# Delta rule in a hybrid streaming encoder: the triangular inverse built by whole-array products on the transposed matrix

## What is computed

```python
G = jnp.cumsum(gc, axis=-1)
decay_in = jnp.exp(jnp.where(causal, G[..., :, None] - G[..., None, :], -jnp.inf))
kk = jnp.einsum('nbhid,nbhjd->nbhij', kc, kc)
M = jnp.where(strict, bc[..., :, None] * kk * decay_in, 0.0)
rhs = jnp.concatenate([bc[..., None] * vc, (bc * jnp.exp(G))[..., None] * kc], axis=-1)
sol = lax.linalg.triangular_solve(M + eye, rhs, left_side=True, lower=True)
...
def step(S, xs):
    u = u_v_n - jnp.einsum('bhld,bhdv->bhlv', w_k_n, S)
    o = jnp.einsum('bhld,bhdv->bhlv', q_dec_n, S) + jnp.einsum('bhij,bhjv->bhiv', qk_n, u)
    S = S * g_last_n[..., None, None] + jnp.einsum('bhld,bhlv->bhdv', k_dec_n, u)
```

## Time and profile before

| | |
|---|---|
| three runs | 1804.99, 1807.17, 1808.63 us (median 1807.17) |
| profiled execution | 1809.03 us, of which span 1807.1 us |
| mean granted TensorE clock | 0.97 |
| PE, PEld busy | 93%, 80% of the span |
| DVE, ACT, POOL busy | 59%, 42%, 9% |
| the delta-rule phase | from about 75 us to about 750 us |

### The profile page before, as it was taken

How to read it: one execution, slowest core, us unless ns; L and a number is a source line. 1 busy time by engine, 2 the same in 40 slices (tenths; PEclk the granted TensorE clock), 3 DMA queues, 4 the chain that set the end, 5 groups by cost and what they waited for, 6 DMA issues and landing times. The chain is left out here.

```text
span 1807.1 us, 31679 instructions
## 1 busy us (share of the span) xinstructions
PE 1674.6 (93%) x12005; PEld 1439.7 (80%) x12006; DVE 1066.0 (59%) x2254; ACT 757.6 (42%) x1472; POOL 157.8 (9%) x141
## 2 busy tenths in 40 slices
PE   4799999999999999999998999998999988999990
PEld 2598999999999999887884699998996855666650
DVE  7557857668685875455445311115339976776766
ACT  2555565555556554354444322222113114444434
POOL 0110000000000000100000000000000003444440
PEclk8799999999999999999999999999999989999995
DMA  9521021120202111302116422114123357988866
GB/s 338 184 63 52 25 78 40 52 69 23 79 25 79 39 54 40 117 25 87 61 73 225 169 78 84 46 36 130 48 105 124 143 218 289 322 278 287 246 183 214
DMA packets 69063, 218.09 MB, mean 121 GB/s; under 512 B 9412, under 2 KB 15324, under 8 KB 64324
## 3 DMA queue, kind: packets, MB, share of 16 engines
q1 hardware_dynamic: 61444, 189.02, 29.7%
q0 software_dynamic: 7488, 27.27, 6.3%
HBM read 176.40 MB, written 42.48 MB: 121 GB/s over the span
## 5 line engine op out<-in xcount | busy, mean ns | idle before, releaser
L142 PE MATMUL bk<-hT_high,w_high 128*128 128x352 f32 x840 | 294.9, 351 | 1.1 <-DVE ssq L1303 1.1
L144 PE MATMUL bk<-hT_high,w_low 128*128 128x352 f32 x840 | 272.1, 324 | 0.0
L143 PE MATMUL bk<-hT_low,w_high 128*128 128x352 f32 x840 | 271.8, 324 | 0.0
L142 PEld LDWEIGHTS bk<-hT_high,w_high 128*128 128x128 f32 x840 | 159.7, 190 | 5.3 <-DVE ssq L1303 1.2
L143 PEld LDWEIGHTS bk<-hT_low,w_high 128*128 128x128 f32 x840 | 160.1, 191 | 0.0
L144 PEld LDWEIGHTS bk<-hT_high,w_low 128*128 128x128 f32 x840 | 159.1, 189 | 0.0
L142 PE MATMUL pg<-hT_high,w_high 128*128 128x352 f32 x360 | 116.3, 323 | 0.8 <-PEq L1412 0.8
L143 PE MATMUL pg<-hT_low,w_high 128*128 128x352 f32 x360 | 115.5, 321 | 0.0
L144 PE MATMUL pg<-hT_high,w_low 128*128 128x352 f32 x360 | 115.4, 321 | 0.0
L1084 DVE SCALAR_TENSOR_TENSOR f<-raw,cw,f 128x1059 f32<-128x1059 f32 x72 | 97.1, 1349 | 9.8 <-ACT f L712 8.8
L2730 PE MATMUL psD<-wdn,aTx 128*128 x192 | 86.9, 596 | 2.3 <-DVE ob L2862 1.6
(11 more groups left out here) (489 smaller groups left out, 4149.0 us busy)
## 6 DMA issues: line engine op xcount, KB each, us to landing
wgu<-in_w_gu SPq DMA_DIRECT2D x16, 2048.0 KB, 8.4
wraw<-in_w_gdn SPq DMA_DIRECT2D x32, 512.0 KB, 3.7
wdn<-in_w_dn SPq DMA_DIRECT2D x16, 1024.0 KB, 13.2
wm<-in_w_mod SPq DMA_DIRECT2D x8, 1024.0 KB, 13.3
tmp_x<-x SPq DMA_DIRECT2D x16, 512.0 KB, 3.0
spare<-in_w_mod SPq DMA_DIRECT2D x15, 512.0 KB, 7.9
Dm<-tmp_g_rows SPq DMA_DIRECT2D x8, 576.0 KB, 4.9
EG<-tmp_g_rows SPq DMA_DIRECT2D x8, 576.0 KB, 6.0
```

Source lines behind the costliest of these rows:

```text
L142: pe.matmul(out, lh, rh, start=start, stop=False)
L143: pe.matmul(out, lh, rl, start=False, stop=False)
L144: return pe.matmul(out, ll, rh, start=False, stop=stop)
```

## The change

The inverse is built in another way. C starts as `ET` masked to what lies above the 16x16 diagonal blocks inside each 64x64 quarter (one DVE operation from SBUF, `C_MOFF` changed, no transposes). With the transposed block inverses, the inverse of a quarter is a series in C: Z1 and Z2 each multiply by C and add `RT`, and ZI does the last term for both the inverse (`TT`) and its transpose (`IV`). X and TX make the off-diagonal quarter. All these matmuls have the full 128 rows and 128 columns of weights and 64 moving columns, one per tile, in ZI two. T_ET, BT, B, B2, W, TT and Q are gone; C, Z1, Z2, ZI and X are new, and TX is rewritten. C is the first stage after the slots and waits for `R`. DVE now reads C, Z1, Z2, ZI and X, ACT reads TX, WK and UV. POOL clears two buffers per head. The steps of `fill` are shared out by weights (`SHARE`), 42 in a steady iteration as before. The diff, cut to its core:

```diff
-    A2 = ("QK", "BT", "B", "B2", "W", "TT", "T_O", "Q", "T_V", "TX", "WK", "UV")
+    A2 = ("C", "Z1", "Z2", "ZI", "QK", "T_O", "X", "T_V", "TX", "WK", "UV")
+    SHARE = {"C": 5, "Z1": 5, "Z2": 5, "ZI": 4, "QK": 3, "T_O": 3, "X": 4, "T_V": 3, "TX": 4, "WK": 3, "UV": 4}
...
-    after_stage = {"QK": 2, "W": 3}
+    after_stage = {"C": 2, "QK": 3}
...
+                def zeros(a):
+                    if a > 0:
+                        pool.wait_ge(s["o"], NCHUNK * a)
+                    pool.memset(XL[:, :], 0.0)
+                    pool.memset(IV[:, :], 0.0).then_inc(s["zero"], 1)
...
+                def series(lhsT, rhs):
+                    return lambda t, out: pe.matmul(out, tl(lhsT, t), rhs(t), start=True, stop=True)
                 def inverses(t, out):
-                    mul2(R, A1T)(t, out)
-                    return corner(hl(A1T, 0, t), hl(R, 0, t), out[:, HB2:P], 0)
+                    pe.matmul(out[:, 0:HB2], tl(C, t), ptl(Z2, t), start=True, stop=True)
+                    return pe.matmul(out[:, HB2:P], ptl(Z2, t, P), tl(C, t)[:, 0:HB2], start=True, stop=True)
                 def upper(t, out):
-                    return corner(tl(TT, t)[HALVES[0], HALVES[1]], hl(Q, 0, t), out, 0)
+                    return pe.matmul(out, ptl(XL, t, P), tl(TT, t)[:, HALVES[1]], start=True, stop=True)
...
-                    evacuated(pe, a, "KK")
-                    stage(a, "T_ET", turn(ET))
...
+                    if name == "C":
+                        pe.wait_ge(s["nt"], a + 1)
+                        pe.wait_ge(s["r"], a + 1)
+                        stage(a, "C", series(C, lambda t: htl(R, t)), HB2)
+                    if name == "Z1":
                         pe.wait_ge(s["rt"], a + 1)
+                        stage(a, "Z1", series(C, lambda t: htl(RT, t)), HB2)
+                    if name == "Z2":
+                        stage(a, "Z2", series(C, lambda t: htl(Z1, t)), HB2)
+                    if name == "ZI":
+                        pe.wait_ge(s["zero"], a + 1)
+                        stage(a, "ZI", inverses)
+                    if name == "X":
+                        stage(a, "X", series(ET, lambda t: htl(IV, t)), HB2)
...
-                    for g in range(NGRP):
-                        off_diagonal(a, g)
+                    evacuated(dve, a, "KK")
+                    dve.tensor_tensor(by_tile(C), by_tile(ET), c.consts[:, C_MOFF, :].unsqueeze(1).to_broadcast([P, TILES, P]),
+                                      ALU.mult).then_inc(s["nt"], 1)
...
+                        if name == "C":
+                            for g in range(NGRP):
+                                src = halves(take_from(dve, a, "C", g)[:, 0:G3 * HB2])
+                                dve.tensor_tensor(grp3(C, g)[up, :, up], src[up, :, :], rows_scaled(a, g)[up, :, :], ALU.mult)
+                                dve.tensor_tensor(grp3(C, g)[low_, :, low_], src[low_, :, :], rows_scaled(a, g)[low_, :, :],
+                                                  ALU.mult).then_inc(free[g], 1)
+                        if name == "ZI":
+                            dve.wait_ge(s["r"], a + 1)
+                            for g in range(NGRP):
+                                src = take_from(dve, a, "ZI", g)[:, 0:W3].rearrange("p (t n) -> p t n", n=P)
+                                rt, r = halves(hgrp(RT, g)), halves(hgrp(R, g))
+                                dve.tensor_tensor(halves(hgrp(IV, g))[up, :, :], src[up, :, HB2:P], r[up, :, :], ALU.add)
+                                dve.tensor_tensor(grp3(TT, g)[up, :, up], src[up, :, 0:HB2], rt[up, :, :], ALU.add)
+                                dve.tensor_tensor(grp3(TT, g)[low_, :, low_], src[low_, :, 0:HB2], rt[low_, :, :],
                                                   ALU.add).then_inc(free[g], 1)
```

More of the change, by code:

```diff
@@ L507, in stage_steps @@
         left = start(h + 1) - start(h) - after_slots(h)
-        return left * (i + 1) // len(A2) - left * i // len(A2)
+        upto = [sum(SHARE[name] for name in A2[:n]) for n in (i, i + 1, len(A2))]
+        return left * upto[1] // upto[2] - left * upto[0] // upto[2]
     def subs_done(h, done):
@@ L516, in phase_deltanet @@
         a = h + 1
-        order = ([] if a == HA else ["KK", "T_ET", "SQ", "T_K"]) + \
+        order = ([] if a == HA else ["KK", "SQ", "T_K"]) + \
                 [s for s in A2 if (a < HA or s == "T_O") and (h >= 0 or s != "T_O")]
@@ L585, in hgrp, with htl, pgrp, ptl @@
             return m[:, g * G3 * HB2:(g + 1) * G3 * HB2]
-        def hl(m, b, t):
-            return m[HALVES[b], t * HB2:(t + 1) * HB2]
+        def htl(m, t):
+            return m[:, t * HB2:(t + 1) * HB2]
+        def pgrp(m, g):
+            return m[:, g * WP:g * WP + G3 * HB2]
+        def ptl(m, t, n=HB2):
+            lo = t // G3 * WP + t % G3 * HB2
+            return m[:, lo:lo + n]
+        def halves(ap):
+            return ap.rearrange("p (t n) -> p t n", n=HB2)
         def hby(m):
@@ L846, in _ @@
                                 evacuate(a, "UV", UV)
-                            if stage == "Q" and a + 1 < HA:
+                            if stage == "T_V" and a + 1 < HA:
                                 tap(a + 1, KB)
-                        if h >= 0 and stage == "B2":
+                        if h >= 0 and stage == "ZI":
                             act.wait_ge(s["ms"], h + 1)
@@ L1103, in eliminate @@
                     st.link(dve.tensor_tensor(m, m, out, ALU.add))
[L1105 to L1111, removed]
                 def low(w):
@@ L1194, in combine, with rows_scaled, plus_rt @@
                         dve.tensor_tensor(grp(dst, g), src[:, 0:W3], grp(other, g), op).then_inc(free[g], 1)
-                def combine_halves(a, stage, dst, other, op):
+                def rows_scaled(a, g):
+                    return c1[:, G3 * g:G3 * g + G3].unsqueeze(2).to_broadcast([P, G3, HB2])
+                def plus_rt(a, stage, dst):
                     for g in range(NGRP):
                         src = take_from(dve, a, stage, g)
-                        dve.tensor_tensor(hgrp(dst, g), src[:, 0:G3 * HB2], hgrp(other, g), op).then_inc(free[g], 1)
+                        dve.tensor_tensor(dst(g), src[:, 0:G3 * HB2], hgrp(RT, g), ALU.add).then_inc(free[g], 1)
@@ L1210, in second @@
+                        if name == "X":
+                            for g in range(NGRP):
+                                src = halves(take_from(dve, a, "X", g)[:, 0:G3 * HB2])
+                                dve.tensor_tensor(halves(pgrp(XL, g))[low_, :, :], src[low_, :, :], rows_scaled(a, g)[low_, :, :],
+                                                  ALU.mult).then_inc(free[g], 1)
                         if name == "T_V":
@@ L1239, in second, with output @@
                             dve.tensor_tensor(WE[:, :, P:2 * P], by_tile(f[QB]), by_tile(EG), ALU.mult).then_inc(s["eq"], 1)
-                    if h < 0:
-                        return
-                    if name == "BT":
+                    if h >= 0:
+                        output(h, name)
+                    if a < HA and name in V_TAPS:
+                        tap(a, VB, 1 + V_TAPS.index(name))
+                V_TAPS = ("ZI", "QK", "T_O")
+                def output(h, name):
+                    if name == "Z1":
                         dve.wait_ge(s["o_taken"], NCHUNK * (h + 1) + 2)
```

100 lines of the change are left out of this document (22 added, 78 removed).

## The result

| | before | after |
|---|---|---|
| median of the runs | 1807.1 us (1805.0 to 1808.6) | 1882.6 us (1879.3 to 1887.7) |
| profiled execution, span | 1809.0, 1807.1 us | 1882.3, 1880.5 us |
| mean granted TensorE clock | 0.970 | 0.955 |
| end of the delta-rule phase | 755.0 us | 829.9 us |

The change makes the kernel 4.2% slower: ratio 1.042 (95% interval 1.0406 to 1.0434). That is 75.5 us, where 65 were forecast; 1882.6 lies in the range of 1845 to 1896, and just above the 1862 to 1882 that the forecast gave as its own. The phase's end moves by 74.9 us, so what follows it takes as long as before (1052.1 and 1050.6 us).

A forecast was written before the change was run, and what follows sets the result against it. PE was taken to bound the delta-rule phase. Work, waits at C, clock falls and DVE's tie gave 7.8 us per steady head, 67 in all, less about 2: +65 on 1807.2, 1872 us; 80% range 1845 to 1896, own range 1862 to 1882.

The forecast's parts named there:

- PE bounds the phase: Delta-rule phase: PE is busy for all 78.5 us of a steady iteration, so its added work and waits lengthen the kernel.
- Work, +2.8 us a head: PE's stages per head: 14.5 us of new matmuls added against 11.65 us removed or replaced.
- The rivals of 0.072 and 0.032 us: Cheaper records in the new stages: loads partly hidden, 1833 us, chance 0.07; pace set by moving columns, 1792 us, chance 0.05.
- Waits at C, 30 us: PE waits for `R` at C: 3.3 us in six steady iterations, 5.3 in the first, 5.1 in the last.
- The clock, 12 us: Granted clock falls after each of the eight waits at C, 1.5 us each, 12 us in all.
- its upper bound of 24: Upper bound of the clock term after the waits at C, with falls twice as long; the lower bound was 0.
- I count 1.5 us for each: Each of eight waits at C brings 3.4 us at half pace, costing some 1.5 us.
- DVE's tie: From ZI to X, PE and DVE both need 8.1 us; 0.2 us counted per steady head.
- The sum: Whole phase: six steady heads 47 us, first 10.5, last 9.7; 67 less about 2 of old waits, +65 us.

The follow-up runs named there:

- experiment 4: Kernel before, with only its QK made to wait for `R`, which it does not use: 1844.7 us, ratio 1.02.
- experiment 10: Experiment 9 with two taps of the values one stage earlier, from ZI to Z2 and from Z2 to Z1: 1798.0 us, ratio 0.9937 to the kernel before.
- experiment 5: Changed kernel with the wait for `R` filled by surplus products whose output is never read: 1863.1 us, ratio 1.0302 to the kernel before.
- experiment 1: Changed kernel with QK ahead of C again, taps and splits where the kernel before had them: 1849.3 us, ratio 1.0239 to the kernel before.
- experiment 2: Changed kernel, same order, with all products of C, Z1, Z2, ZI, X and TX on 64x64 quarters: 1840.2 us, ratio 1.0183 to the kernel before.
- experiment 3: Changed kernel with both QK ahead of C and the series products on 64x64 quarters: 1818.6 us, ratio 1.0053 to the kernel before.
- experiment 7: Experiment 3 with `R` copied ahead of `RT` on ACT: 1810.8 us, ratio 1.0012 to the kernel before.
- experiment 8: Experiment 7 with T_O moved behind X, the last tap of the values at X and their silu at T_O: 1818.8 us, ratio 1.0049.
- experiment 9: Experiment 7 with the output's norm put ahead of ZI's readings on DVE: 1811.8 us, ratio 1.0018 to the kernel before.
- experiment 11: Experiment 10 with DVE's weight split also moved from ZI to Z2: 1805.0 us, ratio 0.9977 to the kernel before.

## Why the prediction held, and where it was off

- **PE bounds the phase.** Held: PE's work, its waiting and the clock together account for the shift of the phase's end, in the change (below) and in experiment 4, where 27 us more of idle PE and 12.6 of the clock stand against 39 at the end. Experiment 10 shows it from the other side.
- **Work, +2.8 us a head.** Held. A clean iteration of the change is 84.56 us (experiment 5); less the 3.18 us in which C could not start, it is 2.8 us above the 78.55 of before, from the norm's product (L959) in one iteration to the next (work and the tie at X together; 3.0 were forecast). The single stages take 2.01 us where 2.08 was forecast, ZI 4.02 where 4.1 was. Against that the removed work was counted 0.2 us too high: Q and TX have half the records of B, and Q to T_V is 3.21 us with four steps, so they take 1.29 us and not 1.39. The two errors nearly cancel. A record costs 0.107 to 0.111 us for 64 moving columns, as for 128: QK's stage takes 2.01 as well. The rivals of 0.072 and 0.032 us are out. The Trainium skill ("TensorE: Matmul & The Clock Gate", section "LDWEIGHTS (loading the stationary operand)") puts the load of 128 columns at 107 ns; the single stages agree.
- **Waits at C, 30 us.** Held: 29.4 us, 3.18 steady, 5.22 first, 5.04 last (3.3, 5.3, 5.1 forecast). That the matrix would be late followed from one change of order, and experiment 1 undoes it.
- **The clock, 12 us.** This is the term that was mis-sized. It came to 26 us, just over its upper bound of 24: experiment 5 gives back 12.6 us in the six steady iterations, 8.0 in the first and 5.5 in the last, where 9, 1.5 and 1.5 were forecast. The price of a stretch was right: 3.4 us at the lower clock cost 1.5 us. What failed is the step "I count 1.5 us for each", which took one length for all. The eight stretches were 20.5, 3.4, 6.8, 3.4, 6.8, 3.4, 3.4 and 13.7 us, 61.4 in all. In 3.1 us of the first and 2.0 of the last PE was still waiting for C; the other 56.3 us at 0.46 each (86.18 and 87.74 against 84.56 for 3.4 and 6.8) are the 26. The bound was no bound either: it allowed twice the length, and the first wait's was six times it. That 12 us are possible with the same waits is seen in experiment 4; which of the two it would be, no row of before could tell. The first stretch, 20.4 us at 0.50 with the last 3 us of the wait in it:

```profile
143.80:164.20 20.40, 17.35 (x76) 17.38 (x77) 5.50 (x13) 5.84 (x14) 2.35 (x1) 0.50 0.14 49
```

- **DVE's tie.** Held for the change, whose wait at X is too small for the list of waits in a steady iteration; DVE is busy for 60.96 us in one, where 60 was forecast (4.2 us more than before by the sum, 5.7 measured). As soon as the stages were shorter or the waits at C gone, PE waited for DVE, or for ACT behind it, at T_O, X or T_V: in experiments 1 to 3, 7 to 9 and 11. Only experiment 10 is free of it in a steady iteration.
- **The sum.** 22.6 us are work (eight heads at 2.83), 27.0 are idle time of PE (35.1 in the phase against 8.1; 29.4 at C, 2.4 less elsewhere) and 26 are the clock, 76 together; the phase is 75.8 us longer (it starts 0.9 us earlier and ends 74.9 later). By iteration, the six steady ones grew by 47.0 us, and 47 were forecast, though that is in part luck: 0.6 us more a head for the clock stood against 0.3 less for waits and work and some old waits that went. The first grew by 15.6 and the last by 14.3, where 10.5 and 9.7 were forecast. There, in the longest stretches at the lower clock, lies nearly all of the miss.

The change itself has two parts of opposite worth. The series with the mask needs no transposes and fewer stages, and on quarters it saves 2.2 us a head (76.35 against 78.55, both with PE busy throughout). On whole arrays it costs 2.8, and with C first it brings the waits and the clock.

## What to carry to other kernels

Price a small fp32 product by its weight columns, not by its moving ones (0.107 us a record for 128 weight columns, with 64 moving columns as with 128): where the operand is block-diagonal, two half-size products side by side can beat one of full size. A stage that heads the program order of the bounding engine must not wait for what was produced last; put one that needs nothing ahead of it. A wait on TensorE costs its length and, sometimes, a stretch at half the clock that can be longer than the wait: for a forecast, the number and the length of these stretches are the wide part of the range.

## What the runs showed of the hardware that was not expected

- **Falls of the clock are not a function of the wait's length.** Idle times of 3.1 to 3.2 us in steady iterations brought a fall in 6 of 6 (the change), 5 of 6 (experiment 2), 3 of 6 (4). 1.36 us brought three of six, 0.89 us three of six, 1.07 us none of six (experiment 7), 1.42 us none of six (experiment 8). The stretches were 3.4, 6.8, 10.2, 13.7 or 20.5 us long.
- **DVE and POOL hold each other up, whoever starts second.** In the change an operation of DVE with both inputs in SBUF takes 2.92 us where it starts inside a subtraction of POOL:

```profile
435.77 2.38 POOL L858 TENSOR_TENSOR w_low<-wraw,w_high 128x1024 fp32r<-128x1024 f32 x1 [37.91 <-ACT w_high L690]
```

```profile
436.45 2.92 DVE L1224 TENSOR_TENSOR WE<-f,EG 128x1152 f32<-128x1152 f32 x1 [1.24 <-PE bk L934]
```

In experiment 10 DVE starts first, and then POOL is the one that is held up:

```profile
467.36 3.48 POOL L858 TENSOR_TENSOR w_low<-wraw,w_high 128x1024 fp32r<-128x1024 f32 x1 [28.73 <-ACT w_high L690]
```

```profile
467.26 1.36 DVE L1235 TENSOR_TENSOR WE<-f,EG 128x1152 f32<-128x1152 f32 x1
```

The Trainium skill ("SBUF — State Buffer", section "Who interferes with whom") says that a DVE instruction with two inputs in SBUF shares a read port with a GpSimd instruction that reads SBUF, and that whoever issues first keeps the port for its whole instruction while the other is blocked. The numbers agree to within 0.2 us: DVE takes 1.56 us more (2.92 for 1.36) where POOL had 1.70 left to go, and POOL 1.10 more (3.48 for 2.38) where DVE had 1.26. Neither shows in the list of PE's waits.
